# A gated DeltaNet layer: the low products of a weight tile last, and no products with the zero state of a head's first chunk

## The chip, the cores and the metric

The kernel runs on one core of a Trainium2 chip. The metric is the device time of one execution in microseconds (us). Engines: TensorE (PE) multiplies, VectorE (DVE), ScalarE (ACT) and GpSimd (POOL) work elementwise, SyncE (SP) issues the DMAs.

## The reference

DEPTH is 1, so the one layer is the gated DeltaNet: 1024 tokens, width 1024, 8 heads with keys of 128 and values of 256, all in float32.

```python
h = rms_norm(x, norm_w) * (1 + scale) + shift          # shift, scale, gate from c
qkv, z, b, a = split(h @ w_in)
q, k, v = split(silu(causal_short_conv(qkv, conv_w)))   # q, k l2-normed per head
def step(S, inp):                                       # per head, chunk by chunk
    v_new = u_c - w_c @ S
    o_c = q_c @ S + attn_c @ v_new
    S = S * gl_c + k_c.T @ v_new
    return S, o_c
S0 = zeros                                              # the state of a head's first chunk
y = (rms_norm(o, norm_w) * silu(z)) @ w_out
out = rms_norm(x + gate * y, final_norm_w)
```

u and w come from a triangular solve within each chunk: (I + A)^-1 with A from k k^T, the decay and beta.

## The kernel before

Work is cut into 16 units: unit u = 2 hd + par is one half (512 tokens, four chunks of 128) of head hd. The even unit (par 0) is the first half, so its chunk 0 starts with the zero state; the odd unit goes on with the state of the even one. A unit has six tiles of the input projection (k, z0, z1, q, v0, v1; some for the next unit): `project` (L396) computes tile m as h (1024 x 512) by 128 weight columns in bank m % 2, as 24 products of 128x128 by 128x512. Full precision comes from splits into a high and a low part: for each of the eight k, w_hi h_hi, w_hi h_lo and w_lo h_hi. The weight tile lands in w_raw, two slots, loaded by SP. ACT makes w_hi by a rounding copy (L685, `split_hi`), POOL makes w_lo as the difference, in four operations (L1344, `split_lo`), and frees the slot. On even units POOL also scales and splits the two halves of the head's output weights (L1358, L1351), and SP loads these in between.

The order of every engine is written out by hand. On PE (`body`, L511), `fill(n)` puts the next n products of the projection between the dependent steps. Per unit: the merges of the block inverses (`merge_p`, `merge_d`), k and v of the next and this unit turned, then per chunk c:

- ks (L538) = k_c state and qs (L542) = q_c state, each in two passes in the profile;
- fill, x (L550) = u_fin r, where r = v - e ks is DVE's L1107;
- fill, kv (L560) and av (L563), from xs (ACT's scaled x, L756);
- fill. In chunk 0 the fills have 8, 8 and 6 products (`FILLS`, L257), and tile 3 (n = 72) begins with the first of them.

DVE in an even unit (`body`, L1071), behind make_n (L992) for the next unit: memset of the state (L1100), r (L1107), a silu (L947), and the inversion of the next unit's 16x16 blocks, cut into `BASE_STEPS` (L262). Three of its steps, two small operations each (L1007, L1011), come in chunk 0 before the state's update (L1124) and o (L1130), then a silu and three more steps, then r of chunk 1. The inversion's input goes through DRAM: SP, in `body` (L348), waits for wo_lo of the second output half, loads tile 4, then in `invert_out` (L287) stores nmat to n_dram (L289), waits until that has landed and reads it back as blocks (L291). ACT (`body`, L776) in chunk 0: scaled q state (L750), z evacuated (L703, L706), scaled x (L756), then w_hi of tile 4.

Semaphores count per unit: `passed(engine, name, u, n)` waits for the n-th event of that name in unit u. `UNIT` (L155) has the counts: state_done 5 per unit, the first by the memset, or in the odd unit by an increment alone.

Of the kernel before, what the change touches and what calls it, by code (L numbers as in the profile page):

```python
# [7 lines left out]
ALU = mybir.AluOpType  # L8
ACT = mybir.ActivationFunctionType

P = 128
# [4 lines left out]
DV = 256  # L16
# [3 lines left out]
KT = D_MODEL // P  # L20
# [19 lines left out]
def build(nc, x, c, ada_w, ada_b, norm_w, w_in, conv_w, a_log, dt_bias, gdn_norm_w, w_out,  # L40
          final_norm_w, out):
    ctx = ExitStack()
    with ctx:
# [32 lines left out]
        neg_egc = sb("neg_egc", [P, UNITS, NCH])  # L76
        e_kd = sb("e_kd", [P, UNITS, NCH])
        e_gl = sb("e_gl", [P, UNITS, NCH])
# [13 lines left out]
        state = sb("state", [P, DV])  # L92

        def part(at, n, **dims):
# [3 lines left out]
        cvk = part(0, 1024, to="p (s t) -> p s t", s=2)  # L98
# [20 lines left out]
        r_rhs = part(10752, DV)  # L119
# [39 lines left out]
            base_step=32, base_done=1, t_done=1,  # L159
            merge_p=3, merge_p_out=3, merge_d=3, merge_d_out=3,  # L160
            ks_done=4, qs_done=4, r_done=4, qs_scaled=4, x_done=4, x_out=4,
            kv_done=4, av_done=4, state_done=5, o_done=4, o_squared=4, o_step=4, o_pow=4,
            o_turned=4, og_done=4, og_hi_done=4, og_lo_done=4, out_done=4, y_added=4,
        )
        HEAD = ("wo_gated", "wo_hi_done", "wo_lo_done")
# [45 lines left out]
        def passed(eng, name, u, n):  # L211
            value = at(name, u, n)
            if not isinstance(value, int) or value > 0:
                eng.wait_ge(S[name], value)
# [178 lines left out]
        def _(pe):  # L393
            prime(pe, "tensor")

            def project(u, par, first, last, final=False):  # L396
                first_unit = isinstance(u, int) and u == -1
                for n in range(first, last):
                    m, r = divmod(n, MM)
                    k, part_no = divmod(r, 3)  # L400
                    if r == 0:
                        passed(pe, "w_lo_done", u, m + 1)
                        passed(pe, "evacuated", u, m - 1)
                    half = par if final or (m in (1, 2) and not first_unit) else 1 - par
                    w, h = ((w_hi, h_hi_v), (w_hi, h_lo_v), (w_lo, h_hi_v))[part_no]
                    mm = nc.tensor.matmul(bank[m % 2][:, :], w[:, m % 2, k, :], h[:, k, half, :],  # L406
                                          start=(r == 0), stop=(r == MM - 1))
                    if r == MM - 1:
                        mm.then_inc(S["projected"], 1)
# [101 lines left out]
            def body(hd, par, last=False, begun=0, fills=FILLS):  # L511
# [20 lines left out]
                fill(in_v)  # L532

                for c in range(NCH):
                    passed(pe, "state_done", u, c + 1)
                    if c == 0:
                        passed(pe, "v_scaled", u, 4)
                    nc.tensor.matmul(bank[2][:, 0:DV], cvk[:, par, c * P:(c + 1) * P], state[:, :],  # L538
                                     start=True, stop=True).then_inc(S["ks_done"], 1)
                    passed(pe, "og_done", u, max(c - 1, 0))  # L540
                    passed(pe, "qs_scaled", u, c)
                    nc.tensor.matmul(bank[3][:, 0:DV], cvq[:, par, c * P:(c + 1) * P], state[:, :],  # L542
                                     start=True, stop=True).then_inc(S["qs_done"], 1)
                    if c >= 2:
                        out_project(u, c - 2, 0, hd, par, not last)
                    fill(in_chunk[c][0])
                    if c == 0:
                        passed(pe, "merge_d_out", u, 3)
                    passed(pe, "r_done", u, c + 1)
                    nc.tensor.matmul(bank[4][:, 0:DV], u_fin[:, c, :], r_rhs, start=True, stop=True  # L550
                                     ).then_inc(S["x_done"], 1)
                    if c >= 2:
                        out_project(u, c - 2, 1, hd, par, not last)
                    fill(in_chunk[c][1])
# [123 lines left out]
        def _(act):  # L678
# [97 lines left out]
            def body(hd, par, last=False, first=False):  # L776
# [22 lines left out]
                    split_hi(u, hd, par, 3)  # L799
                scale_v(u, par)  # L800
                for c in range(NCH):
                    scale_q(u, c)
                    if not last:
                        if c == 0:
                            evacuate_z(u, 2, 1)
# [102 lines left out]
        def _(dve):  # L908
# [162 lines left out]
            def body(hd, par, last=False, first=False):  # L1071
# [23 lines left out]
                    k_scalars(u + 1, other)  # L1095
                    make_n(u + 1, other)

                if par == 0:
                    passed(dve, "qs_done", u, 0)
                    nc.vector.memset(state[:, :], 0.0).then_inc(S["state_done"], 1)  # L1100
                else:
                    dve.sem_inc(S["state_done"], 1)
                for c in range(NCH):
                    passed(dve, "ks_done", u, c + 1)
                    passed(dve, "v_scaled", u, c + 1)
                    passed(dve, "x_done", u, c)
                    stt(out=r_rhs, in0=bank[2][:, 0:DV], scalar=neg_egc[:, u, c:c + 1], in1=vt[:, c, :],  # L1107
                        op0=ALU.mult, op1=ALU.add).then_inc(S["r_done"], 1)
                    if c == 0:
                        if last:  # L1110
                            silu(u, 1, zt[:, 1, :], gate=True)
# [8 lines left out]
                    if c > 0:  # L1120
                        gate_o(u, c - 1)
                    passed(dve, "kv_done", u, c + 1)
                    passed(dve, "qs_done", u, c + 1)
                    stt(out=state[:, :], in0=state[:, :], scalar=e_gl[:, u, c:c + 1], in1=bank[4][:, DV:2 * DV],  # L1124
                        op0=ALU.mult, op1=ALU.add).then_inc(S["state_done"], 1)
                    passed(dve, "av_done", u, c + 1)
                    passed(dve, "qs_scaled", u, c + 1)
                    passed(dve, "o_turned", u, c - 1)
                    passed(dve, "o_squared", u, c - 1)
                    nc.vector.tensor_tensor(o_raw[:, c % 2, :], bank[5][:, 0:DV], qss, ALU.add  # L1130
                                            ).then_inc(S["o_done"], 1)
                    if c >= 2:
                        add_y(u, par, c - 2)
                    if not last:
# [346 lines left out]
```

## Time and profile before

| | |
|---|---|
| Median of 3 runs | 1201.96 us (1201.87 to 1202.51) |
| The profiled execution | 1203.63 us, its span 1201.8 us |
| PE busy | 1114.4 us, 93% of the span |
| DVE, ACT, POOL busy | 836.7, 448.1, 599.9 us (70, 37, 50%) |
| Mean granted TensorE clock | 0.972 |
| Longest chain | PE 64%, POOL 12%, DVE 11%, issue 7% |
| DMA | 87.73 MB on the one queue, 26.6% of its engines' time |

Busy time is the sum over an engine's instructions in the profile. The chain is followed back from the last instruction to what released each step. Idle time is put down to the instruction whose semaphore came last; idle of an engine that is not the bound costs nothing by itself.

### The profile page before, as it was taken

The page shows a single profiled execution, that of the slowest core. Times are in us where ns is not written, and L with a number is a line of the kernel's source. Part 1 is how long each engine was busy: PE and PEld are TensorE (multiplying, and loading weights), DVE is VectorE, ACT ScalarE, POOL GpSimd, SP SyncE. Part 2 cuts the span into 40 slices and gives each one's busy share as a digit, 9 for nine tenths or more (in the row PEclk, how much of TensorE's full clock was granted, in tenths as well). Part 3 has the DMA queues.
Part 4 walks back from the last instruction along what each step waited for, and adds up shares of the span by engine and source line. Part 5 has one row for each costly group of instructions (what it writes and reads, how often), then busy time and mean ns, then how long its engine had stood idle before and what let it go on. Part 6 is the DMA issues. An engine that isn't in the chain of part 4 may idle for free.

```text
span 1201.8 us, 19507 instructions
## 1 busy us (share of the span) xinstructions
PE 1114.4 (93%) x5628; PEld 920.6 (77%) x5628; DVE 836.7 (70%) x1888; ACT 448.1 (37%) x1038; POOL 599.9 (50%) x819
## 2 busy tenths in 40 slices
PE   3896899999999999999999999999999999999984
PEld 2665688887888788887888788887888788887863
DVE  4776586776858586775858586685868677685835
ACT  4642333333242433433333333334243333334333
POOL 2353544565444744466345754456444853456413
PEclk9897899999999999999999999999999999999988
DMA  9922222213122321223221221223221222213103
GB/s 311 326 58 60 63 58 62 55 57 81 40 62 57 80 57 44 56 60 76 55 62 40 81 65 43 62 55 81 57 59 43 79 56 55 62 40 97 33 25 123
DMA packets 150754, 88.31 MB, mean 73 GB/s; under 512 B 29446, under 2 KB 145320, under 8 KB 150696
## 3 DMA queue, kind: packets, MB, share of 16 engines
q1 hardware_dynamic: 150696, 87.73, 26.6%
q14 instruction: 45, 0.37, 0.1%
q8 instruction: 13, 0.21, 0.1%
HBM read 78.28 MB, written 9.44 MB: 73 GB/s over the span
## 4 chain that ended last, share of the span: by engine, by line
PE 64%; POOL 12%; DVE 11%; issue 7%; ACT 2%; DMA 1%; SPq 0%; DVEq 0%; POOLq 0%; ACTq 0%
PE bank L406 31%; PE bank L506 11%; POOL w_lo L1344 5%; POOL wo_lo L1351 4%; DVE y L963 3%; DVE work L930 3%; PE bank L550 2%; PE bank L466 2%; PE bank L560 2%; PE bank L538 2%; PE bank L542 2%; PE bank L482 2%; PE bank L475 2%; PE bank L563 2%; PE bank L588 1%
## 5 line engine op out<-in xcount | busy, mean ns | idle before, releaser
L1344 POOL TENSOR_TENSOR w_lo<-w_raw,w_hi 128x256 fp32r<-128x256 f32 x384 | 333.5, 898 | 254.9 <-ACT w_hi L685 254.8
L406 PE MATMUL bank<-h_hi,w_hi 128*128 128x512 f32 x760 | 320.2, 421 | 20.8 <-POOL w_lo L1344 20.8
L406 PE MATMUL bank<-h_lo,w_hi 128*128 128x512 f32 x760 | 313.4, 412 | 0.0
L406 PE MATMUL bank<-h_hi,w_lo 128*128 128x512 f32 x760 | 310.6, 409 | 0.0
L406 PEld LDWEIGHTS bank<-h_hi,w_hi 128*128 128x128 f32 x760 | 146.5, 193 | 53.7 <-POOL w_lo L1344 24.8
L930 DVE SCALAR_TENSOR_TENSOR work<-pre,cw,work 128x512 f32<-128x512 f32 x192 | 168.5, 878 | 14.1 <-DVE work L927 5.4
L406 PEld LDWEIGHTS bank<-h_hi,w_lo 128*128 128x128 f32 x760 | 145.6, 192 | 30.8 <-issue 0.2
L406 PEld LDWEIGHTS bank<-h_lo,w_hi 128*128 128x128 f32 x760 | 146.9, 193 | 27.8 <-issue 0.2
L1394 POOL TENSOR_TENSOR og_lo<-work,og_hi 128x256 fp32r<-128x256 f32 x64 | 47.1, 737 | 217.4 <-ACT og_hi L745 217.4
L711 ACT ACTIVATE work<-work 128x512 f32<-128x512 f32 x64 | 40.2, 628 | 271.8 <-DVE pre L940 131.0
L506 PE MATMUL bank<-wo_hi,og_hi 128*128 128x512 f32 x256 | 113.7, 444 | 10.1 <-DVE y L963 10.1
L963 DVE SCALAR_TENSOR_TENSOR y<-bank,o_rs,y 128x512 f32<-128x512 f32 x128 | 89.5, 739 | 23.4 <-PE bank L506 23.4
L1007 DVE TENSOR_TENSOR work<-work 32x15 f32<-32x15 f32 (+7 forms) x240 | 70.1, 292 | 47.0 <-DMA work<-n_dram 39.2
L685 ACT ACTIVATE w_hi<-w_raw 128x1024 fp32r<-128x1024 f32 x96 | 101.2, 1054 | 1.6 <-DMA w_raw<-in_gdn_w_in 1.6
L506 PE MATMUL bank<-wo_hi,og_lo 128*128 128x512 f32 x256 | 100.7, 393 | 0.0
L506 PE MATMUL bank<-wo_lo,og_hi 128*128 128x512 f32 x256 | 100.3, 392 | 0.0
L947 DVE SCALAR_TENSOR_TENSOR work<-work 128x512 f32<-128x512 f32 x96 | 76.7, 799 | 3.2 <-ACT work L711 1.4
L756 ACT ACTIVATE work<-bank,k_tab 128x256 f32<-128x256 f32 x64 | 30.4, 475 | 116.4 <-PE bank L550 116.4
L954 DVE SCALAR_TENSOR_TENSOR work<-bank,small,work 128x128 f32<-128x128 f32 x128 | 38.7, 342 | 50.1 <-PE bank L491 50.1
L745 ACT ACTIVATE og_hi<-work 128x256 fp32r<-128x256 f32 x64 | 26.7, 417 | 115.6 <-DVE work L954 112.6
L506 PEld LDWEIGHTS bank<-wo_hi,og_hi 128*128 128x128 f32 x256 | 48.0, 188 | 24.1 <-POOL og_lo L1394 14.2
L1011 DVE TENSOR_TENSOR work<-work 32x15 f32<-32x15 f32 (+7 forms) x240 | 60.1, 250 | 8.3
(176 smaller groups left out, 1870.0 us busy)
## 6 DMA issues: line engine op xcount, KB each, us to landing
w_raw<-in_gdn_w_in SPq DMA_DIRECT2D x96, 512.0 KB, 4.0
work<-in_ada_w SPq DMA_DIRECT2D x8, 1024.0 KB, 9.7
w_raw<-in_gdn_w_out SPq DMA_DIRECT2D x16, 512.0 KB, 3.3
y<-in_x SPq DMA_DIRECT2D x8, 512.0 KB, 9.1
work<-in_ada_w SPq DMA_DIRECT2D x8, 512.0 KB, 6.1
n_dram<-work SPq DMA_DIRECT2D x16, 256.0 KB, 3.4
out<-y SPq DMA_DIRECT2D x8, 512.0 KB, 2.7
t_dram<-work SPq DMA_DIRECT2D x16, 64.0 KB, 1.6
```

The source lines that it names most:

```text
L406: mm = nc.tensor.matmul(bank[m % 2][:, :], w[:, m % 2, k, :], h[:, k, half, :], start=(r == 0), stop=(r == MM - 1))
L506: mm = nc.tensor.matmul(bank[6 + n][:, :], a[:, m, :], w[:, m, n * 512:(n + 1) * 512], start=(m == 0 and q == 0), stop=(m == 1 and q == 2))
L685: nc.scalar.activation(w_hi[:, k % 2, :, :], w_raw_k[:, k % 2, :, :], ACT.Copy).then_inc(S["w_hi_done"], 1)
L711: nc.scalar.activation(th[:, m % 2, :], cv, ACT.Tanh, scale=0.5).then_inc(S["tanh_done"], 1)
L930: o = stt(out=cv, in0=pre[:, r, j:j + HALF], scalar=tap, in1=cv, op0=ALU.mult, op1=ALU.add)
L947: stt(out=t, in0=th[:, m % 2, :], scalar=1.0, in1=t, op0=ALU.add, op1=ALU.mult).then_inc(S["silu_done"], 1)
L963: i = stt(out=yt, in0=bank[6 + n][:, :], scalar=o_rs[:, c:c + 1], in1=yt, op0=ALU.mult, op1=ALU.add)
L1007: nc.vector.tensor_tensor(tmp, blk_n[:, j:j + 1, j + 1:].rearrange("p o n -> p n o").to_broadcast(shape), blk_y[:, j:j + 1, 0:j + 1].to_br ...
L1011: nc.vector.tensor_tensor(below, below, tmp, ALU.subtract).then_inc(S["base_step"], 1)
L1344: i = nc.gpsimd.tensor_tensor(w_lo[:, k % 2, j:j + 2, :], w_raw_k[:, k % 2, j:j + 2, :], w_hi[:, k % 2, j:j + 2, :].bitcast(F32), ALU.subt ...
L1351: o = nc.gpsimd.tensor_tensor(wo_lo[:, i, j:j + 256], w_raw[:, 1 - i, j:j + 256], wo_hi[:, i, j:j + 256].bitcast(F32), ALU.subtract)
L1394: nc.gpsimd.tensor_tensor(og_lo[:, :, :], og, og_hi[:, :, :].bitcast(F32), ALU.subtract).then_inc(S["og_lo_done"], 1)
```

## The change

In `project` the 24 products of a tile come in another order: first, for each k, w_hi h_hi and w_hi h_lo (r = 0 to 15), then for each k w_lo h_hi (r = 16 to 23). At r = 0 PE waits for w_hi and the bank, and only at r = 16 for w_lo. In the first chunk of an even unit ("fresh") ks and qs are left out, x takes the scaled v in place of r, DVE makes no r and no memset, and copies kv to the state and av to o; ACT leaves out the scaled q state. Semaphores are incremented instead where something counts them. state_done has 4 events a unit.

```diff
--- before.py
+++ after.py
@@ -159,7 +159,7 @@
             base_step=32, base_done=1, t_done=1,
             merge_p=3, merge_p_out=3, merge_d=3, merge_d_out=3,
             ks_done=4, qs_done=4, r_done=4, qs_scaled=4, x_done=4, x_out=4,
-            kv_done=4, av_done=4, state_done=5, o_done=4, o_squared=4, o_step=4, o_pow=4,
+            kv_done=4, av_done=4, state_done=4, o_done=4, o_squared=4, o_step=4, o_pow=4,
             o_turned=4, og_done=4, og_hi_done=4, og_lo_done=4, out_done=4, y_added=4,
         )
         HEAD = ("wo_gated", "wo_hi_done", "wo_lo_done")
@@ -397,10 +397,13 @@
                 first_unit = isinstance(u, int) and u == -1
                 for n in range(first, last):
                     m, r = divmod(n, MM)
-                    k, part_no = divmod(r, 3)
+
+                    k, part_no = divmod(r, 2) if r < 2 * KT else (r - 2 * KT, 2)
                     if r == 0:
+                        passed(pe, "w_hi_done", u, m + 1)
+                        passed(pe, "evacuated", u, m - 1)
+                    elif r == 2 * KT:
                         passed(pe, "w_lo_done", u, m + 1)
-                        passed(pe, "evacuated", u, m - 1)
                     half = par if final or (m in (1, 2) and not first_unit) else 1 - par
                     w, h = ((w_hi, h_hi_v), (w_hi, h_lo_v), (w_lo, h_hi_v))[part_no]
                     mm = nc.tensor.matmul(bank[m % 2][:, :], w[:, m % 2, k, :], h[:, k, half, :],
@@ -532,23 +535,29 @@
                 fill(in_v)
 
                 for c in range(NCH):
-                    passed(pe, "state_done", u, c + 1)
+                    fresh = par == 0 and c == 0
                     if c == 0:
                         passed(pe, "v_scaled", u, 4)
-                    nc.tensor.matmul(bank[2][:, 0:DV], cvk[:, par, c * P:(c + 1) * P], state[:, :],
-                                     start=True, stop=True).then_inc(S["ks_done"], 1)
-                    passed(pe, "og_done", u, max(c - 1, 0))
-                    passed(pe, "qs_scaled", u, c)
-                    nc.tensor.matmul(bank[3][:, 0:DV], cvq[:, par, c * P:(c + 1) * P], state[:, :],
-                                     start=True, stop=True).then_inc(S["qs_done"], 1)
+                    if fresh:
+                        pe.sem_inc(S["ks_done"], 1)
+                        pe.sem_inc(S["qs_done"], 1)
+                    else:
+                        passed(pe, "state_done", u, c)
+                        nc.tensor.matmul(bank[2][:, 0:DV], cvk[:, par, c * P:(c + 1) * P], state[:, :],
+                                         start=True, stop=True).then_inc(S["ks_done"], 1)
+                        passed(pe, "og_done", u, max(c - 1, 0))
+                        passed(pe, "qs_scaled", u, c)
+                        nc.tensor.matmul(bank[3][:, 0:DV], cvq[:, par, c * P:(c + 1) * P], state[:, :],
+                                         start=True, stop=True).then_inc(S["qs_done"], 1)
                     if c >= 2:
                         out_project(u, c - 2, 0, hd, par, not last)
                     fill(in_chunk[c][0])
                     if c == 0:
                         passed(pe, "merge_d_out", u, 3)
-                    passed(pe, "r_done", u, c + 1)
-                    nc.tensor.matmul(bank[4][:, 0:DV], u_fin[:, c, :], r_rhs, start=True, stop=True
-                                     ).then_inc(S["x_done"], 1)
+                    if not fresh:
+                        passed(pe, "r_done", u, c + 1)
+                    nc.tensor.matmul(bank[4][:, 0:DV], u_fin[:, c, :], vt[:, 0, :] if fresh else r_rhs,
+                                     start=True, stop=True).then_inc(S["x_done"], 1)
                     if c >= 2:
                         out_project(u, c - 2, 1, hd, par, not last)
                     fill(in_chunk[c][1])
@@ -799,7 +808,10 @@
                     split_hi(u, hd, par, 3)
                 scale_v(u, par)
                 for c in range(NCH):
-                    scale_q(u, c)
+                    if par == 0 and c == 0:
+                        act.sem_inc(S["qs_scaled"], 1)
+                    else:
+                        scale_q(u, c)
                     if not last:
                         if c == 0:
                             evacuate_z(u, 2, 1)
@@ -1095,17 +1107,17 @@
                     k_scalars(u + 1, other)
                     make_n(u + 1, other)
 
-                if par == 0:
-                    passed(dve, "qs_done", u, 0)
-                    nc.vector.memset(state[:, :], 0.0).then_inc(S["state_done"], 1)
-                else:
-                    dve.sem_inc(S["state_done"], 1)
                 for c in range(NCH):
-                    passed(dve, "ks_done", u, c + 1)
-                    passed(dve, "v_scaled", u, c + 1)
-                    passed(dve, "x_done", u, c)
-                    stt(out=r_rhs, in0=bank[2][:, 0:DV], scalar=neg_egc[:, u, c:c + 1], in1=vt[:, c, :],
-                        op0=ALU.mult, op1=ALU.add).then_inc(S["r_done"], 1)
+
+                    fresh = par == 0 and c == 0
+                    if fresh:
+                        dve.sem_inc(S["r_done"], 1)
+                    else:
+                        passed(dve, "ks_done", u, c + 1)
+                        passed(dve, "v_scaled", u, c + 1)
+                        passed(dve, "x_done", u, c)
+                        stt(out=r_rhs, in0=bank[2][:, 0:DV], scalar=neg_egc[:, u, c:c + 1], in1=vt[:, c, :],
+                            op0=ALU.mult, op1=ALU.add).then_inc(S["r_done"], 1)
                     if c == 0:
                         if last:
                             silu(u, 1, zt[:, 1, :], gate=True)
@@ -1120,15 +1132,22 @@
                     if c > 0:
                         gate_o(u, c - 1)
                     passed(dve, "kv_done", u, c + 1)
-                    passed(dve, "qs_done", u, c + 1)
-                    stt(out=state[:, :], in0=state[:, :], scalar=e_gl[:, u, c:c + 1], in1=bank[4][:, DV:2 * DV],
-                        op0=ALU.mult, op1=ALU.add).then_inc(S["state_done"], 1)
+                    if fresh:
+                        passed(dve, "qs_done", u, 0)
+                        nc.vector.tensor_copy(state[:, :], bank[4][:, DV:2 * DV]).then_inc(S["state_done"], 1)
+                    else:
+                        passed(dve, "qs_done", u, c + 1)
+                        stt(out=state[:, :], in0=state[:, :], scalar=e_gl[:, u, c:c + 1], in1=bank[4][:, DV:2 * DV],
+                            op0=ALU.mult, op1=ALU.add).then_inc(S["state_done"], 1)
                     passed(dve, "av_done", u, c + 1)
-                    passed(dve, "qs_scaled", u, c + 1)
                     passed(dve, "o_turned", u, c - 1)
                     passed(dve, "o_squared", u, c - 1)
-                    nc.vector.tensor_tensor(o_raw[:, c % 2, :], bank[5][:, 0:DV], qss, ALU.add
-                                            ).then_inc(S["o_done"], 1)
+                    if fresh:
+                        nc.vector.tensor_copy(o_raw[:, 0, :], bank[5][:, 0:DV]).then_inc(S["o_done"], 1)
+                    else:
+                        passed(dve, "qs_scaled", u, c + 1)
+                        nc.vector.tensor_tensor(o_raw[:, c % 2, :], bank[5][:, 0:DV], qss, ALU.add
+                                                ).then_inc(S["o_done"], 1)
                     if c >= 2:
                         add_y(u, par, c - 2)
                     if not last:
```

PE, chunk 0 of an even unit in the loop, before: from ks to x ("..." stands for six more products of the tile).

```order
L538 MATMUL bank<-state,work 128x256 [waits v_scaled,state_done]
L542 MATMUL bank<-state,work 128x256 [waits qs_scaled,og_done]
L214 REGISTER_ALU
L406 MATMUL bank<-h_hi,w_hi 128x512 [waits evacuated,w_lo_done]
L406 MATMUL bank<-h_lo,w_hi 128x512
L406 MATMUL bank<-h_hi,w_lo 128x512
...
L214 REGISTER_ALU [waits merge_d_out]
L550 MATMUL bank<-work 128x256 [waits r_done]
```

And with the change, from the wait for the scaled v to ks of chunk 1:

```order
L214 REGISTER_ALU [waits v_scaled]
L409 MATMUL bank<-h_hi,w_hi 128x512 [waits evacuated,w_hi_done]
L409 MATMUL bank<-h_lo,w_hi 128x512
...
L559 MATMUL bank<-work 128x256 [waits merge_d_out]
...
L569 MATMUL bank<-work 128x256 [waits kdec_done,x_out]
L572 MATMUL bank<-work 128x256 [waits o_done]
L409 MATMUL bank<-h_hi,w_lo 128x512 [waits w_lo_done]
L409 MATMUL bank<-h_hi,w_lo 128x512 x5
L546 MATMUL bank<-state,work 128x256 [waits state_done]
```

L538 and L542 are gone from this place; the wait for w_lo_done stands behind L569 and L572 (L560 and L563 of before), on the first of the six products of the third fill, and the next wait is L546's for state_done.

DVE, the same chunk, before: from make_n to the first inversion step.

```order
L992 SCALAR_TENSOR_TENSOR work<-bank,k_tab,work 128x128 x3
L1100 MEMSET state 128x256 [waits qs_done]
L1107 ISA [waits x_done,v_scaled,ks_done]
L1107 SCALAR_TENSOR_TENSOR work<-bank,neg_egc,work 128x256
...
L947 SCALAR_TENSOR_TENSOR work<-work 128x512 [waits evacuated,tanh_done]
...
L214 REGISTER_ALU [waits blk_in]
L1007 TENSOR_TENSOR work<-work 32x15 [waits base_step]
```

And with the change, from make_n to o:

```order
L1004 SCALAR_TENSOR_TENSOR work<-bank,k_tab,work 128x128 x3
...
L959 SCALAR_TENSOR_TENSOR work<-work 128x512 [waits evacuated,tanh_done]
...
L214 REGISTER_ALU [waits blk_in]
L1019 TENSOR_TENSOR work<-work 32x15 [waits base_step]
...
L1023 TENSOR_TENSOR work<-work 32x13x3 [waits base_step]
L1137 COPY state<-bank 128x256 [waits qs_done,kv_done]
L214 REGISTER_ALU [waits av_done]
L1146 COPY work<-bank 128x256 [waits o_squared,o_turned]
```

The memset and r, and their waits, are gone; the wait for blk_in (the reload of n_dram) and the inversion's six operations stand ahead of the state's copy as they stood ahead of its update.

## Rows read from the trace of the kernel before

**Rows 1.** Who waited for whom: us in total, times, longest (us).
```profile
DVE work L1007 <- DMA work<-n_dram: 39.2, 8, 5.2
...
PE bank L406 <- POOL w_lo L1344: 20.8, 10, 2.3
```

**Rows 2.** Timeline of PE, u = 8 (start us, us, engine line op, idle before).
```profile
547.15 0.60 PE L538 MATMUL bank<-state,work 128*128 128x256 f32 x2
...
550.46 0.80 PE L406 MATMUL bank<-h_hi,w_hi 128*128 128x512 f32 x1 [2.29 <-POOL w_lo L1344]
...
558.44 0.60 PE L538 MATMUL bank<-state,work 128*128 128x256 f32 x2
...
561.16 0.65 PE L550 MATMUL bank<-work 128*128 128x256 f32 x2
```

**Rows 3.** Windows, two even units (length, engines' busy, PEclk, DMA, GB/s).
```profile
550.30:553.60 3.30, 3.14 (x7) 2.51 (x8) 0.00 (x0) 0.00 (x0) 0.11 (x1) 0.50 0.52 145
1096.30:1099.60 3.30, 3.23 (x8) 2.55 (x9) 0.00 (x0) 0.00 (x0) 0.02 (x1) 0.52 0.46 130
```

**Rows 4.** Timeline of PE in an odd unit, u = 7.
```profile
480.55 0.60 PE L538 MATMUL bank<-state,work 128*128 128x256 f32 x2
...
481.64 0.40 PE L406 MATMUL bank<-h_lo,w_hi 128*128 128x512 f32 x1
481.88 0.40 PE L406 MATMUL bank<-h_hi,w_lo 128*128 128x512 f32 x1
...
487.79 0.59 PE L538 MATMUL bank<-state,work 128*128 128x256 f32 x2
```

**Rows 5.** Timeline of DVE in u = 8.
```profile
554.38 0.17 DVE L1007 TENSOR_TENSOR work<-work 32x15 f32<-32x15 f32 x1 [4.82 <-DMA work<-n_dram]
...
555.44 0.19 DVE L1011 TENSOR_TENSOR work<-work 32x39 f32<-32x39 f32 x1
556.91 0.48 DVE L1124 SCALAR_TENSOR_TENSOR state<-state,e_gl,bank 128x256 f32<-128x256 f32 x1 [1.29 <-PE bank L560]
...
558.63 0.72 DVE L1007 TENSOR_TENSOR work<-work 32x48 f32<-32x48 f32 x1
...
560.57 0.48 DVE L1107 SCALAR_TENSOR_TENSOR work<-bank,neg_egc,work 128x256 f32<-128x256 f32 x1
```

**Rows 6.** Timeline of POOL in u = 8.
```profile
544.40 2.84 POOL L1351 TENSOR_TENSOR wo_lo<-w_raw,wo_hi 128x256 fp32r<-128x256 f32 x4
...
556.04 3.26 POOL L1344 TENSOR_TENSOR w_lo<-w_raw,w_hi 128x256 fp32r<-128x256 f32 x4 [5.63 <-ACT w_hi L685]
```

**Rows 7.** SP's issues in u = 8; the first's time to landing (last row, us).
```profile
547.26 0.38 SPq L269 DMA_DIRECT2D w_raw<-in_gdn_w_in  x1
547.75 0.52 SPq L289 DMA_DIRECT2D n_dram<-work  x1
552.36 0.34 SPq L291 DMA_DIRECT2D work<-n_dram  x1
...
w_raw<-in_gdn_w_in SPq DMA_DIRECT2D x1, 512.0 KB, 4.4
```

**Rows 8.** Timeline of ACT in u = 8.
```profile
554.91 1.05 ACT L685 ACTIVATE w_hi<-w_raw 128x1024 fp32r<-128x1024 f32 x1
```

**Rows 9.** Timeline of DVE in an odd unit, u = 7; POOL's L1344 ends at 498.62.
```profile
497.35 0.67 DVE L1011 TENSOR_TENSOR work<-work 32x60 f32<-32x60 f32 x1
...
498.73 0.20 DVE L1011 TENSOR_TENSOR work<-work 32x55 f32<-32x55 f32 x1
```

**Rows 10.** Timeline of PE in the start, and the window 122 to 123 us.
```profile
83.20 0.51 PE L406 MATMUL bank<-h_hi,w_hi 128*128 128x512 f32 x1 [1.68 <-POOL w_lo L1344]
...
110.43 1.97 PE L466 MATMUL bank<-work 128*128 128x64 f32 x8 [7.49 <-DVE work L1028]
114.16 0.79 PE L406 MATMUL bank<-h_hi,w_hi 128*128 128x512 f32 x1 [1.76 <-POOL w_lo L1344]
...
122.00:123.00 1.00, 1.00 (x7) 0.99 (x5) 0.00 (x0) 0.00 (x0) 1.00 (x2) 0.50 0.07 12
```

## The prediction

> **What bounds the kernel now.** I began with the page: TensorE (PE) is busy nearly all of the span, so the time is what PE's stream costs plus its waits. Next came the list of who waited for whom [rows 1]. PE waited 20.8 us in 10 waits for GpSimd's low half of a weight tile (L1344), and VectorE (DVE) 39.2 us in 8 waits for the reload of n_dram.
>
> The timeline of PE in the even unit of one head, u = 8 [rows 2], shows the stall: behind the two products with the state (the first at 547.15), 2.29 us pass until tile 3's first product. The same stands in all eight even units; two of the ten waits lie in the start (1.68 and 1.76 us [rows 10]), so the eight have (20.8 - 3.44) / 8 = 2.17 us on the mean. The windows [rows 3] add what idle time hides: behind the stall the granted clock is 0.50 (1.2 of 2.4 GHz) for 3.3 us, in the last such unit as in this one. At half clock 1.65 us of work are lost. A stall costs 2.17 + 1.65.
>
> **The change, part by part.** In PE's order the low products of a tile, and their wait, come behind the sixteen high ones. Tile 3's then stand behind L560 and L563 of chunk 0.
> - Stall. PE reaches them at about 552.1 (547.15 and the odd unit's spacing, less the state products). w_lo(3) is there by 550.46 [rows 2], so this stall goes, with 1.6 us to spare. w_hi(3) is no new wait: ScalarE makes it ahead of the scaled v that PE waits for at this place already.
> - State products. They cost 1.09 us from 480.55 to 481.64, less one normal product (0.24, 481.64 to 481.88): 0.86 us [rows 4].
> - With no other wait, ks of chunk 1 would come 7.24 us (480.55 to 487.79 in the odd unit, which has no stall) less 0.86 behind 547.15: at 553.53, against 558.44 now. That is 4.91 us earlier per head, if nothing else is late.
>
> **What is late next.** ks of chunk 1 reads the state, and DVE writes the state behind the first three inversion steps of the next unit, which wait for n_dram [rows 5]. They start at 554.38 and end at 555.63; the state follows at 556.91, since it waits 1.29 us for L560. The slack is that 1.3 us, not 4.9. And 554.38 doesn't move. SP issues tile 4's load at 547.26, when POOL's wo_lo (L1351) ends at 547.24 [rows 6], then n_dram's store at 547.75, and the reload when that has landed, at 552.36 [rows 7]. All of this starts ahead of the part of PE's stream that gets shorter. So the stall moves to L546 (L538 of before).
>
> **A collision.** Now w_hi(4) starts at 554.91, behind L550's result [rows 8], and POOL's w_lo(4) at 556.04, when the three steps are done [rows 6]. With L550 at about 549, ScalarE waits only for the tile, landed 4.4 us behind its issue [rows 7]: w_hi(4) 551.7 to 552.8, w_lo(4) 552.9 to 555.7. The three steps then run beside POOL. In the odd unit such an operation beside L1344 takes 0.67 us, and 0.20 when POOL is done [rows 9]. The Trainium skill ("GPSIMD Engine Reference", Specifications) says that GpSimd shares its SBUF interfaces with VectorE and contends with instructions that have two SBUF inputs. By that rule the steps are held and the state's, from PSUM, is not; the trace agrees (0.72 against 0.48 for L1124, both beside L1344) [rows 5].
> Bounds of the delay: 0 (POOL done first), and all six operations at 0.68 instead of 0.21, 2.8 us. I take two held turns, 1.2 us, since POOL would be in the last two of its four operations.
>
> **The sum for a head.** Steps end at 556.85, the state takes 0.48 (at most, L1124's), 0.1 to start: ks at 557.4, 1.04 us earlier than now. PE has stood since 553.7: 3.7 us. The eight stalls of about 2.2 us halved the clock, so this one does: 1.65 us lost. From ks to L550 are 2.72 us (558.44 to 561.16), so L550 of chunk 1 is at 561.8, not 561.16: **+0.6 us**. DVE's r (560.57 now, 3.66 behind the state's start, of which 0.8 was spent beside POOL) is there at 560.3 and doesn't bind. Two additions. DVE no longer waits for ks and runs its silu beside POOL's last wo_lo operation, on which the DMA chain hangs: bounds 0 and 0.3, I take 0.1. And the clock can stay low longer: in the start it still stood at 0.50 at 122 us though PE worked from 114.16 on [rows 10]; here a longer gap can reach into the slow stretch in the same way. Bounds 0 and 1.65; one head in five, 0.3 on the mean. Together +1.0 us, for 7 heads **+7.0**.
>
> **The start and the rest.** The wait at 83.20 is worth nothing, since PE then waits 7.49 us for DVE at 110.43. The 1.76 us at 114.16 go, and the merge products behind them start what DVE does next: -1.8, to -3 if the clock comes back sooner [rows 10]. In the first even unit I take 0. The reordered products are the same in number and kind. The removed memset, scale and r of the first chunk lie in the shadow of the DMA; the added semaphore increments on PE, ACT and DVE lie ahead of the new gap, so at up to a few tenths each they cost nothing.
> Sum: 7.0 - 1.8 = +5.2 us. The profiled execution took 1203.63 (span 1201.8); the median of the runs, 1201.96, lies 1.7 lower, and the sum is added to it: **1207.0 us** (A).
>
> **Rivals.**
> - **B, gain.** POOL's w_lo(4) doesn't hold the steps: ks at 556.2, gap 2.5, clock halved, L550 at 560.57. That is -0.6 for 8 heads, start -2.4: 1194.8. For it: 1.2 us is my choice between 0 and 2.8. Against: the tile lands 0.7 us ahead of n_dram, and the reload takes 2 us more. It decides below some 0.6 us of delay.
> - **B2, as B with the clock kept.** r at 559.9 then holds L550: -1.3 for 8 heads, start -2.4: 1189.2. At 83.20 a gap of 1.68 us was followed by a product of 0.51 us, at 550.46 one of 2.29 by 0.80 [rows 2, 10], and this gap would be the longer. The Trainium skill ("TensorE: Matmul & The Clock Gate", Why this matters for your kernels) warns only of gaps longer than all eight stalls. By that rule B2 would stand in B's place; the clock of all eight speaks against it.
> - **D, a second slow stretch in every head.** +0.6 + 0.1 + 1.5 for 7 heads, less 1.8: 1215.6.
> - **N, they cancel.** Delay 0.7: ks at 556.9, with the additions +0.2 for 8 heads, start -1.8: 1201.8.
> - **F, nothing is late next.** 8 (2.17 + 1.65 + 0.86) = 37.4, start 2.4: 1162.2. That the change doesn't move the wait is excluded by the order; for its whole gain the reload would have to land 3 us sooner.
>
> **How the numbers follow.** Chances: A 0.48 (its own range 1203 to 1211), B 0.17, B2 0.08, D 0.12, N 0.12, F 0.03. "Same" is within 0.2%, 2.4 us, about what a measurement of this kernel can tell. Slower: 0.44 of A and D, 0.56. Same: 0.04 of A and 0.11 of N. Faster: B, B2, F and 0.01 of N, 0.29. The range leaves out B2, F and the upper half of D: 1194 to 1215. Both signs hold weight, since 0.6 us per head changes them.
>
> **What would show it.** The waits of PE's projection for L1344 fall from 10 to 1 or 0. In their place stand 8 waits of the state product for DVE's state copy, 3.3 to 4 us each, and a DVE idle of 6 to 7 us ahead of the inversion's first step, still ended by n_dram. L1344 for tile 4 starts some 1.5 us ahead of that step, and the first two operations take 0.5 to 0.7 us. The clock is 0.50 behind each gap. It is wrong if the gap is under 2.7 us (B), if the clock stays at 1.00 (B2), if operations beside POOL take 0.2 us, or if PE waits at L550's successor in chunk 1 for r instead.

## The result and the profile after

| | before | after |
|---|---|---|
| Median of the runs taken together | 1201.87 us (5 runs, 1200.05 to 1202.51) | 1207.0 us (5 runs, 1206.86 to 1207.17) |
| Profiled execution, its span | 1203.63, 1201.8 us | 1206.86, 1204.4 us |
| PE busy | 1114.4 us | 1108.6 us |
| POOL, DVE busy | 599.9, 836.7 us | 600.9, 833.0 us |
| Mean granted clock | 0.972 | 0.971 |

The ratio is 1.0046 (95% interval 1.0036 to 1.0057): slower by 5 us, though PE's busy time fell by 5.8 us.

Who waited for whom, after (us in total, times, longest), against [rows 1]:

```profile
PE bank L546 <- DVE state L1137: 25.1, 8, 3.8
...
PE bank L469 <- DVE work L1040: 9.2, 1, 9.2
...
DVE work L1019 <- DMA work<-n_dram: 56.6, 8, 7.5
```

No product of the projection waits for w_lo any more. Its 20.8 us in 10 waits are replaced by 25.1 us in 8, of the second chunk's ks (L546) for the state that DVE copies (L1137). DVE's idle ahead of the reload has grown from 39.2 to 56.6 us.

PE after, single products left out, against [rows 2]. It is the same even unit, the fourth, at about 550 us; by the kernel's own count from 0 that is u = 6, not 8 as the rows ahead call it (and their odd unit is u = 5), and it is called u = 6 from here on:

```profile
547.73 0.60 PE L559 MATMUL bank<-work 128*128 128x256 f32 x2
...
550.68 1.74 PE L409 MATMUL bank<-h_hi,w_lo 128*128 128x512 f32 x6
555.91 1.22 PE L546 MATMUL bank<-state,work 128*128 128x256 f32 x2 [3.50 <-DVE state L1137]
...
561.20 0.92 PE L559 MATMUL bank<-work 128*128 128x256 f32 x2
```

The low products run at 550.68 without a wait, and PE then stands 3.50 us. In the seven heads from u = 2 to u = 14 the gap is 3.39 to 3.79 us, in the first even unit (145.67) 0.34.

DVE, POOL, ACT and SP in the same unit, against [rows 5 to 8]:

```profile
544.92 0.85 DVE L959 SCALAR_TENSOR_TENSOR work<-work 128x512 f32<-128x512 f32 x1
...
553.53 0.45 DVE L1019 TENSOR_TENSOR work<-work 32x15 f32<-32x15 f32 x1 [7.36 <-DMA work<-n_dram]
554.01 0.65 DVE L1023 TENSOR_TENSOR work<-work 32x15 f32<-32x15 f32 x1
554.70 0.18 DVE L1019 TENSOR_TENSOR work<-work 32x28 f32<-32x28 f32 x1
...
555.34 0.19 DVE L1023 TENSOR_TENSOR work<-work 32x39 f32<-32x39 f32 x1
555.45 0.41 DVE L1137 COPY state<-bank 128x256 f32<-128x256 f32 x1
```

```profile
543.07 3.29 POOL L1370 TENSOR_TENSOR wo_lo<-w_raw,wo_hi 128x256 fp32r<-128x256 f32 x4
546.32 2.81 POOL L1363 TENSOR_TENSOR w_lo<-w_raw,w_hi 128x256 fp32r<-128x256 f32 x4
551.86 2.77 POOL L1363 TENSOR_TENSOR w_lo<-w_raw,w_hi 128x256 fp32r<-128x256 f32 x4 [2.72 <-ACT w_hi L694]
```

```profile
550.72 1.06 ACT L694 ACTIVATE w_hi<-w_raw 128x1024 fp32r<-128x1024 f32 x1 [1.88 <-DMA w_raw<-in_gdn_w_in]
```

```profile
546.38 0.38 SPq L269 DMA_DIRECT2D w_raw<-in_gdn_w_in  x1
546.87 0.52 SPq L289 DMA_DIRECT2D n_dram<-work  x1
551.45 0.34 SPq L291 DMA_DIRECT2D work<-n_dram  x1
```

The first two inversion operations lie in w_lo(4)'s last 1.1 us and take 0.45 and 0.65 us; from 554.70 on, with POOL idle, they take 0.18. The silu (L959), with two small memsets behind it, lies beside wo_lo, which now takes 3.29 us where it took 2.84 [rows 6], and SP's load, store and reload hang on its end.

Windows after, behind the stall of u = 6 and of u = 10, against [rows 3] (length, busy of PE, PEld, DVE, ACT, POOL, then clock, DMA, GB/s):

```profile
555.90:559.30 3.40, 3.38 (x8) 2.72 (x9) 3.09 (x13) 1.41 (x4) 0.73 (x2) 0.50 0.60 152
...
831.60:835.00 3.40, 3.36 (x8) 2.72 (x9) 3.10 (x13) 1.38 (x4) 0.73 (x2) 0.51 0.60 154
```

**One zero of time for all kernels.** ks(c) is the first product with the state in chunk c (L538 before, L546 after). In an even unit DVE's first operation of the k_tab (L978 before, L990 after) lies ahead of all that changed there but the order of the products, so times from its start, E, can be compared: 543.23 before and 541.90 after in u = 6. Means over the seven heads from u = 2 to u = 14:

| us | E to ks(1) | ks(1) to ks(2) | E to the next head's E |
|---|---|---|---|
| before | 15.28 | 7.52 | 136.57 |
| after | 14.10 | 9.49 | 137.63 |

So ks of chunk 1 comes 1.18 us sooner, but at half clock: what follows takes 1.97 us more, for a slow stretch (a time at a granted clock of 0.50) begins around it. In five heads it takes 9.05 to 9.17 us, in u = 6 and u = 12, where the clock stays at 0.50 for 6.8 us instead of 3.4, 10.36 and 10.49. The other 0.3 us lies in the rest of the head. A head costs 1.06 us more.

### The profile page after: what moved, and what is told of

The parts are those of the page before. It is cut to its first block, busy times and chain, and to the rows that moved or that the text cites. A ratio compares the mean times of both kernels' runs of the same rounds, so it can differ in the third digit from the quotient of the medians.

```text
span 1204.4 us, 19318 instructions
## 1 busy us (share of the span) xinstructions
PE 1108.6 (92%) x5596; PEld 914.4 (76%) x5596; DVE 833.0 (69%) x1872; ACT 446.6 (37%) x1030; POOL 600.9 (50%) x819
## 4 chain that ended last, share of the span: by engine, by line
PE 60%; DVE 15%; POOL 10%; issue 6%; DMA 5%; ACT 2%; SPq 1%; DVEq 1%; POOLq 0%; ACTq 0%
PE bank L409 26%; PE bank L509 11%; POOL wo_lo L1370 4%; DVE work L942 3%; DVE y L975 3%; DMA n_dram<-work 3%; PE bank L469 2%; PE bank L546 2%; POOL w_lo L1363 2%; PE bank L559 2%; PE bank L550 2%; PE bank L569 2%; PE bank L485 2%; PE bank L478 2%; POOL w_raw L1377 1%
## 5 line engine op out<-in xcount | busy, mean ns | idle before, releaser
L1363 POOL TENSOR_TENSOR w_lo<-w_raw,w_hi 128x256 fp32r<-128x256 f32 x384 | 326.5, 881 | 232.5 <-ACT w_hi L694 232.5
L409 PE MATMUL bank<-h_hi,w_hi 128*128 128x512 f32 x760 | 329.3, 433 | 2.0 <-ACT work L748 2.0
L409 PE MATMUL bank<-h_lo,w_hi 128*128 128x512 f32 x760 | 302.9, 399 | 0.0
L409 PE MATMUL bank<-h_hi,w_lo 128*128 128x512 f32 x760 | 207.6, 405 | 0.0
L942 DVE SCALAR_TENSOR_TENSOR work<-pre,cw,work 128x512 f32<-128x512 f32 x192 | 168.3, 877 | 14.1 <-DVE work L939 5.4
L1019 DVE TENSOR_TENSOR work<-work 32x15 f32<-32x15 f32 (+7 forms) x240 | 69.1, 288 | 64.6 <-DMA work<-n_dram 56.6
L959 DVE SCALAR_TENSOR_TENSOR work<-work 128x512 f32<-128x512 f32 x96 | 76.2, 794 | 2.9 <-ACT work L720 1.0
L1023 DVE TENSOR_TENSOR work<-work 32x15 f32<-32x15 f32 (+7 forms) x240 | 64.4, 268 | 8.3
L469 PEld LDWEIGHTS bank<-work 128*128 128x128 f32 x384 | 52.0, 197 | 20.2 <-DVE work L1040 9.6
```

The source lines that it names most:

```text
L469: mm = nc.tensor.matmul(p_bank[:, c, :, :], nmat[:, c, :], pairs(tm, lv)[:, c, :, 0, :], start=True, stop=True)
L942: o = stt(out=cv, in0=pre[:, r, j:j + HALF], scalar=tap, in1=cv, op0=ALU.mult, op1=ALU.add)
L959: stt(out=t, in0=th[:, m % 2, :], scalar=1.0, in1=t, op0=ALU.add, op1=ALU.mult).then_inc(S["silu_done"], 1)
L1019: nc.vector.tensor_tensor(tmp, blk_n[:, j:j + 1, j + 1:].rearrange("p o n -> p n o").to_broadcast(shape), blk_y[:, j:j + 1, 0:j + 1].to_br ...
L1023: nc.vector.tensor_tensor(below, below, tmp, ALU.subtract).then_inc(S["base_step"], 1)
L1363: i = nc.gpsimd.tensor_tensor(w_lo[:, k % 2, j:j + 2, :], w_raw_k[:, k % 2, j:j + 2, :], w_hi[:, k % 2, j:j + 2, :].bitcast(F32), ALU.subt ...
```

## The experiments

Each ratio is to the kernel before on the same chip, with its 95% interval. An edit is to the changed kernel where nothing else is said.

**1. low_last**: the kernel before with only the order of the products and their waits changed; the state products stay.

```diff
-                    k, part_no = divmod(r, 3)
+                    k, part_no = divmod(r, 2) if r < 2 * KT else (r - 2 * KT, 2)
```

The waits go with it as in the change, and in the next edit back.

> Only the low products last, with their wait; the products with the zero state stay. Theory A (the state of chunk 0 waits for three inversion steps, these for the reload of n_dram, and the gap before ks of chunk 1 halves the clock): ks and qs are back, so PE comes 0.86 us later to the same gap, 2.3 to 2.8 us instead of 3.5; wo_lo isn't held by the silu, which again waits for ks; POOL's w_lo(4) still runs beside the first steps (+0.75). ks of chunk 1 some 1.5 us earlier than before, 1.65 lost in slow clock: +0.1 to +0.2 us per head, the start -3: 1198 to 1202 us. Rival 1 (the new order of the products costs time by itself): 1207 or more, and mean product times above before's. Rival 2 (a removed stall is simply saved, 2.17 + 1.65 for 8 heads): 1171.

**2. no_zero_state**: only the fresh chunk; the old product order.

```diff
-                    k, part_no = divmod(r, 2) if r < 2 * KT else (r - 2 * KT, 2)
+                    k, part_no = divmod(r, 3)
```

> Only the products with the zero state (and their r, scale and memset) left out, the old order of the products. Theory A: the wait for w_lo(3) takes the 0.86 us back: 8 waits of about 3.0 instead of 2.2 us, clock halved behind them as before, the state behind L560 as before: 1200 to 1204 us. Rival 1: 1202 as well, or less by 7 (0.86 for 8 heads) if those products were on the path: 1195. Rival 2: 1195.

Measured: low_last 1198.4 us, 0.9973 (0.9963 to 0.9983); no_zero_state 1205.54 us, 1.0035 (1.0026 to 1.0045). PE's waits of the one, and of the other:

```profile
PE bank L540 <- DVE state L1126: 18.6, 10, 2.5
```

```profile
PE bank L407 <- POOL w_lo L1361: 25.0, 9, 3.2
```

The order alone replaces the wait for w_lo by one for the state of 2.0 to 2.6 us, with the same 3.4 us at half clock behind it: the loop gains nothing (136.8 us a head against 136.57). What is won lies ahead of it (E of u = 2 at 266.07 us, before at 269.69) and behind it (from E of u = 14 to the end 1.6 us less), where a slow stretch of before is missing in the last unit. The rival that the order itself costs time falls. The fresh chunk alone brings PE 0.9 us sooner to a wait whose end doesn't move: 2.9 to 3.2 us instead of 2.17. What it saves on PE is idle time later. Its result is 1.5 us above its range. In the profiled execution (1206.71 us) one of the seven heads has a slow stretch of 6.8 us, worth 1.4 us; another 1.0 us is lost ahead of u = 2 and 1.0 in the rest of the loop, and for these no cause is shown.

**3. n_first**: in the even units SP stores and reloads n_dram ahead of its wait for wo_lo and of tile 4's load.

```diff
+                    invert_out(u + 1)
                     wo_passed(sp, "wo_lo_done", hd, 2)
                     load_tile(0, v_cols(nxt, 0))
...
-                invert_out(u + 1)
+                    invert_out(u + 1)
```

The last line keeps it in the odd units where it was.

> The changed kernel, and in even units SP stores n_dram and reads it back before it waits for wo_lo and loads tile 4. Theory A: the reload lands at about 549 instead of 553.5, ahead of the kv product, so the gap before ks of chunk 1 goes and with it the slow clock: 4.5 to 6 us per head against the changed kernel, 1160 to 1172 us; mean granted clock 0.99. Rival 1 and any cause in PE's own order or in the added increments: 1205 to 1207. If only the collision with w_lo(4) made the gap: about 1202.

**4. steps_late**: SP as it was; in the even units DVE's first six inversion steps stand behind r of chunk 1.

```diff
+                        if par == 0 and c == 1:
+                            invert_blocks(u + 1, 0, 9)
+                        elif not fresh:
+                            invert_blocks(u + 1, *BASE_STEPS[c])
```

The call for steps 3 to 5, behind chunk 0's second silu, is left to the odd units in the same way.

> The changed kernel, and in even units DVE does the first six inversion steps behind r of chunk 1 instead of in chunk 0; SP's order stays. Theory A: the state is written right behind the kv product, no gap before ks of chunk 1, clock kept; nine steps then stand between r and the state of chunk 1, 4 to 5 us, which may give a wait of up to 1 us before ks of chunk 2: 1160 to 1178 us. Rival 1: 1205 to 1207. If the reload itself were waited for elsewhere on PE: above 1195.

Measured: 1169.76 us, 0.9738 (0.9722 to 0.9754), and 1170.55 us, 0.9746 (0.973 to 0.9763). SP, then PE and DVE of n_first in u = 6:

```profile
537.64 0.38 SPq L289 DMA_DIRECT2D n_dram<-work  x1
539.96 0.34 SPq L291 DMA_DIRECT2D work<-n_dram  x1
```

```profile
543.36 1.73 PE L410 MATMUL bank<-h_hi,w_lo 128*128 128x512 f32 x6
544.93 0.59 PE L547 MATMUL bank<-state,work 128*128 128x256 f32 x2
```

```profile
541.98 0.17 DVE L1020 TENSOR_TENSOR work<-work 32x15 f32<-32x15 f32 x1 [3.20 <-DMA work<-n_dram]
```

One edit brings the reload sooner, the other takes the state out from behind it, and both take away the same stall: ks(1) comes 10.4 us behind E instead of 14.1, with no gap, and the clock stays at 1.00 through the loop. A head takes 132.0 and 132.2 us, and both times lie in their ranges. That the state's place behind the reload makes the stall is shown. Without tile 4's load ahead of it the store is done 2.32 us behind its issue, instead of 4.58 (546.87 to 551.45 above).

**5. n_first_before**: SP's new order in the kernel before.

> The kernel before, with only SP's order changed: in the even units it stores and reloads n_dram ahead of its wait for wo_lo and of tile 4's load. Theory A (in the kernel before the reload hides behind the wait for w_lo(3); it is the change that brings it onto the path): VectorE's idle ahead of the steps falls by about 3 us per head, PE's eight waits for w_lo(3) stay at 2.0-2.3 us, and the time is 1199-1203 us. Rival (the reload bound the kernel before as well): 1185-1195 us.

Measured: 1199.3 us, 0.9984 (0.9972 to 0.9997).

```profile
PE bank L407 <- POOL w_lo L1345: 19.5, 10, 2.6
```

```profile
DVE work L1008 <- DMA work<-n_dram: 7.4, 8, 1.2
```

DVE's idle for the reload falls from 39.2 to 7.4 us, and the time hardly moves: PE waits for w_lo as before. The same edit is worth 2 us here and 37 us in the changed kernel.

**6. lo4_after_state**: POOL makes w_lo(4) of an even unit only when the state is there.

```diff
+                        if par == 0:
+                            passed(pool, "state_done", u, 1)
                         split_lo(u, 4)
```

> The change, and GpSimd waits in the even units for the first chunk's state before it makes w_lo(4), so that no operation of GpSimd lies beside the first six inversion steps. Theory A (the steps are held by w_lo(4), 2.0 us instead of 1.25): the steps take 1.25 us, the stall at ks of chunk 1 falls from 3.4-3.8 to 2.6-3.0 us, and 7 heads save about 0.75 us each: 1200-1204 us, ratio to before 0.998 to 1.002. Rival (the steps are slow for another reason, or ks is bound by something else): unchanged, 1206-1208 us. A gap of 2.7 us should still be followed by a stretch at granted clock 0.50; if it is not, 1190-1194 us.

**7. silu_after_wo**: DVE waits in the fresh chunk for the second wo_lo ahead of its silu.

```diff
+                        if fresh:
+                            wo_passed(dve, "wo_lo_done", hd, 2)
```

> The change, and VectorE waits in the first chunk of the even units for GpSimd's second wo_lo before its silu, so that wo_lo is made alone. Theory A (the silu beside it holds wo_lo, 3.29 us instead of 2.84, and the loads behind it): wo_lo takes 2.84 us, SP's load, n_dram's store and the reload come 0.4 us sooner, and 7 heads save about 0.4 us each: 1202-1206 us. Rival (the chain store-reload is set by the DMA queue, not by wo_lo's end): unchanged, 1206-1208 us.

**8. both_apart**: both waits.

> Both waits: no operation of GpSimd beside the silu or beside the steps. Theory A: the gains add, 1.1 to 1.2 us per head, about 8 us: 1198-1202 us; the stall at ks of chunk 1 is 2.2-2.6 us and the clock behind it is still 0.50. If the clock keeps at 1.00 behind it: 1187-1191 us. Rival (only one of the two matters): 1202-1206 us.

Measured, and from the traces the means over the seven heads:

| | us | ratio | E to ks(1) | a head |
|---|---|---|---|---|
| the change | 1207.0 | 1.0046 (1.0036 to 1.0057) | 14.10 | 137.63 |
| lo4_after_state | 1204.26 | 1.0021 (1.0009 to 1.0033) | 13.31 | 136.81 |
| silu_after_wo | 1205.46 | 1.0027 (1.0012 to 1.0042) | 13.87 | 137.22 |
| both_apart | 1201.16 | 0.9996 (0.9985 to 1.0007) | 13.06 | 136.70 |

Taking the two collisions away gives back 0.8 and 0.2 to 0.4 us a head, and both together 0.93 of the 1.06 us that a head had lost. lo4_after_state ended 0.3 us above its range. But w_lo(4) pushed back falls on DVE's next operations, in both_apart as well: in all seven heads of these two runs r of chunk 1 begins 4.1 us behind ks(1), and 2.2 in the changed kernel. So a collision is moved and not removed, and what the change is worth without any wasn't measured. PE, DVE and the window behind the stall of lo4_after_state in u = 6:

```profile
559.31 0.70 PE L546 MATMUL bank<-state,work 128*128 128x256 f32 x2 [2.89 <-DVE state L1137]
...
563.98 0.70 PE L559 MATMUL bank<-work 128*128 128x256 f32 x2 [1.69 <-DVE work L1119]
```

```profile
560.12 0.73 DVE L1019 TENSOR_TENSOR work<-work 32x48 f32<-32x48 f32 x1
560.88 0.66 DVE L1023 TENSOR_TENSOR work<-work 32x48 f32<-32x48 f32 x1
...
563.44 0.49 DVE L1119 SCALAR_TENSOR_TENSOR work<-bank,neg_egc,work 128x256 f32<-128x256 f32 x1
```

```profile
559.30:563.90 4.60, 2.98 (x12) 2.18 (x12) 4.40 (x10) 1.47 (x4) 4.07 (x6) 1.00 0.03 9
```

Here the clock stays at 1.00, and still nothing is won beyond the collision: r (L1119), held behind four operations of 0.65 to 0.73 us, makes PE wait 1.69 us more. From ks(1) to ks(2) are 9.5 us in the two heads at half clock and in the five at full clock alike. I had expected 0.50 behind these gaps, or 1190 to 1194 us for a clock that is kept. Both were wrong: PE, at full clock, has to wait for r.

**9. n_first_low_last**: the kernel before with n_first's order of SP and low_last's order of the products; the products with the zero state stay, in DVE's and ACT's code too.

> The reordered low products with the zero-state products kept, and SP stores and reloads n_dram ahead of the wait for wo_lo and of tile 4's load. Theory: with the reload sooner the state never binds, so this differs from the full change with the same SP order (1169.8 us) by the state products alone: 8 x 0.86 = 6.9 us, 1175-1178 us, no stall in the loop. Rival (the state products lay in a shadow there, worth nothing): 1169-1171 us. If the later memset and state of this version bind, 1180-1195 us.

Measured: 1182.77 us (1177.85 to 1183.69), 0.9839 (0.9821 to 0.9857).

```profile
PE bank L553 <- DVE work L1110: 6.6, 9, 0.9
```

```profile
545.70 2.82 POOL L1347 TENSOR_TENSOR w_lo<-w_raw,w_hi 128x256 fp32r<-128x256 f32 x4 [4.15 <-ACT w_hi L688]
```

```profile
545.74 0.74 DVE L1014 TENSOR_TENSOR work<-work 32x48 f32<-32x48 f32 x1
546.52 0.67 DVE L1010 TENSOR_TENSOR work<-work 32x55 f32<-32x55 f32 x1
547.22 0.66 DVE L1014 TENSOR_TENSOR work<-work 32x55 f32<-32x55 f32 x1
547.91 0.67 DVE L1010 TENSOR_TENSOR work<-work 32x60 f32<-32x60 f32 x1
548.62 0.21 DVE L1014 TENSOR_TENSOR work<-work 32x60 f32<-32x60 f32 x1
548.85 0.48 DVE L1110 SCALAR_TENSOR_TENSOR work<-bank,neg_egc,work 128x256 f32<-128x256 f32 x1
```

Against n_first the fresh chunk is worth 13 us, not 7: a head takes 133.75 us instead of 131.98. 0.96 us of the difference lie ahead of ks(1), about the two products. Another 1.0 us lies between ks(1) and ks(2), and it is this wait of x(1) for r. The rows of u = 6 show why: w_lo(4) begins 0.1 us behind ks(1) (545.60) and holds four of DVE's operations ahead of r. In n_first PE reaches ks(1) sooner (544.93), w_lo(4) begins 0.8 us behind it, and two are held; over the seven heads it is four each time here and none to two there. The start gives 4 us back (ks(1) of u = 0 at 144.27, in n_first at 148.03). The profiled execution took 1178.84 us, so the traces explain 9 us; what the 4 us more of three of the five runs are stays open.

## Why the prediction was right

The forecast was A, 1207.0 us, and the runs gave 1207.0. That they agree to the tenth is luck: the mechanism in the loop held, but its terms were off by more, in both directions, and the account of the start was wrong.

- **The stall goes.** Right: no wait for w_lo. With w_hi(3) there was no new wait either.
- **It comes back at ks(1), for the state behind the steps.** Right, and shown by n_first and steps_late. Expected were eight gaps of 3.3 to 4 us and a DVE idle of 6 to 7; there are seven of 3.4 to 3.8 and one of 0.34, and the idle is 7.36 in u = 6.
- **554.38 doesn't move.** Off by 0.5 us: in time from E the steps began at 11.15 us and begin at 11.63 (553.53 - 541.90); the means of the seven heads are 11.29 and 11.65. The term that failed is the silu beside wo_lo: I took 0.1, with a bound of 0.3, and it was 0.45 (3.29 against 2.84). In silu_after_wo wo_lo takes 2.84 again and SP's load comes the whole 0.45 us sooner. Only 0.2 us of it arrive at ks(1), since n_dram's store then took 4.84 us on the mean instead of 4.64 until the reload's issue; why is open.
- **The collision of w_lo(4) with the steps.** The mechanism was right, to the operations: POOL began w_lo(4) 1.67 us ahead of the first step (expected: 1.5), and the first two operations were held. The size wasn't: I took 1.2 us for two held turns. The six operations with their gaps took 2.00 us (553.53 to 555.53) instead of 1.25: 0.75 us, and 0.8 on the mean.
- **ks(1) 1.04 us sooner.** It was 1.18, since the two errors above nearly cancel (on the mean the steps began 0.3 us later than I took, and were held 0.4 less).
- **Half clock behind each gap, 1.65 us.** Right: the clock falls to 0.50 in all seven heads of the loop, and costs 1.6 us in five.
- **A second slow stretch in one head of five.** Two of seven, 1.3 us each: 0.4 a head where I took 0.3. D (every head) fell.
- **+1.0 us a head.** +1.06, of which 0.3 lies in the rest of the head, which I had no term for.
- **The start, -1.8, and the first even unit, 0.** Together they are -2.5 (E of u = 2 at 267.16 against 269.69), but it lies the other way round. The wait of 1.76 us for w_lo goes, but PE then stands 4.22 us instead of 1.60 for DVE's silu, and works at half clock again from 125.0 to 131.7 us. So E of u = 0 comes only 0.6 us sooner (133.04 against 133.62), and PE begins chunk 0 there at 137.13 instead of 137.25. The clock doesn't come back sooner in sum either: between 104 and 133 us the mean granted clock is 0.71 both times. The gain is made in the first even unit itself, whose wait of 2.03 us for w_lo and state products are gone while ks(1) waits 0.34 us only, with the clock at 1.00 behind it; part of its chunk 0 ran at half clock ahead of that, which brought PE there later. Before, then after:

```profile
129.53 0.66 PE L415 MATMUL bank<-ident,work 128*128 128x128 f32 x4 [1.60 <-DVE work L947]
137.25 0.67 PE L538 MATMUL bank<-state,work 128*128 128x256 f32 x2 [1.75 <-ACT work L739]
140.38 0.53 PE L406 MATMUL bank<-h_hi,w_hi 128*128 128x512 f32 x1 [2.03 <-POOL w_lo L1344]
```

```profile
126.81 1.11 PE L418 MATMUL bank<-ident,work 128*128 128x128 f32 x4 [4.22 <-DVE work L959]
137.13 0.47 PE L409 MATMUL bank<-h_hi,w_hi 128*128 128x512 f32 x1 [2.05 <-ACT work L748]
145.67 0.70 PE L546 MATMUL bank<-state,work 128*128 128x256 f32 x2 [0.34 <-DVE state L1137]
```

- **The end.** I had no term. In the last unit PE waits 1.75 us for ACT's scaled v before and 1.66 after. Before, the clock is at 0.50 behind it for 6.8 us; after, not. Whether that is the change's doing isn't shown: in no_zero_state the clock fell for 6.8 us behind the same wait of 1.66.

```profile
1157.69 1.01 PE L538 MATMUL bank<-state,work 128*128 128x256 f32 x2 [1.75 <-ACT work L739]
```

```profile
1158.00:1164.00 6.00, 5.43 (x13) 3.25 (x12) 1.98 (x4) 1.26 (x3) 0.00 (x0) 0.50 0.00 0
```

```profile
1161.90 0.70 PE L546 MATMUL bank<-state,work 128*128 128x256 f32 x2 [1.66 <-ACT work L748]
```

```profile
1162.00:1168.00 6.00, 4.66 (x16) 2.52 (x16) 2.47 (x5) 2.70 (x7) 0.84 (x3) 1.00 0.01 1
```

So the spans differ by -2.5 + 6 x 1.06 - 1.3 = +2.6 us, where I had +5.2: six periods lie between the seven heads' E, and the last head with the end gives 1.3 back. The medians differ by 5.1, since the profiled execution of before lay 1.8 us above its median, that of after at its own. One longer slow stretch is worth 1.3 us, half of the difference between the spans, so of the sum only the +1 us a head is shown well, and it has two of them in it.

**The rivals.** B (a gain, w_lo(4) not in the way) decided below 0.6 us of delay; the delay was 0.75. lo4_after_state, with no delay of the steps, gave 1204.26, not 1194.8: ks(1) came 2.0 us sooner than before instead of 2.2, what follows took 2.0 us more instead of 1.65, since r was held, and the rest of the head's 0.3 was missing. B2 (the clock kept) happened in five heads of lo4_after_state and gave nothing there, but with w_lo(4) on r's path, which B2 didn't have; B2 as it was meant stays untested. The Trainium skill ("TensorE: Matmul & The Clock Gate", Why this matters for your kernels) warns only of longer gaps than those of before; all eight of those and low_last's, of 2.0 to 2.6 us, were followed by a clock of 0.50. N's sum is what both_apart measured (1201.16 against 1201.8), though with w_lo(4) moved and not gone. F is n_first: 1169.8, against the 1162.2 worked out for it. In the loop nearly its whole gain was there (4.59 us a head of 4.68), once the reload came sooner, as the prediction said; the first head and what lies ahead of it gave nothing (E of u = 2 at 270.01 us, before at 269.69), where F had some 7.

## What to carry to other kernels

Ahead of taking a wait off the bounding engine, ask of the next operation that it will reach sooner what it needs, and follow that back to what doesn't move: here a DMA that was issued behind an engine's wait, hidden by the stall in question. Try the change together with the edit that moves this cover: alone the two were worth +5 and -2 us, together -31. And where engines are packed against one another, taking out work (the silu's wait for ks) also moves operations onto each other; price each such pair from a pair in the trace, in both directions. Ask also where a group that is pushed away will land: w_lo(4) fell on the first steps in the changed kernel and on those ahead of r in lo4_after_state, both_apart and n_first_low_last.

## What the runs showed of the hardware that was not expected

- The length of a gap doesn't tell whether the clock falls. It fell to 0.50 behind gaps of 2.0 to 2.6 us (low_last, seven of seven) and of 3.4 to 3.8 (after, seven of seven). In lo4_after_state it stayed at 1.00 behind gaps of 2.60 to 2.89 in five of seven heads, and fell behind 2.87 and 2.99; in both_apart it stayed behind gaps of 2.34 and 2.47 and fell behind 2.40 and 2.48; and in the last unit it stayed behind 1.66 us in the changed kernel and fell behind 1.66 in no_zero_state. It doesn't fall at a fixed point of the gap either: in the changed kernel it was 0.50 from 0.8 us ahead of the gap's end on in u = 6 (window 555.10 to 555.90), and still 1.00 for the 0.8 us behind it in u = 14 (1107.13 to 1107.93). A slow stretch in the loop lasted 3.4 or 6.8 us each time. What decides between them is open.
- When VectorE and GpSimd meet, either can be held; what decides isn't shown. A 32x15 operation of DVE took 0.65 us instead of 0.17 and POOL's group 2.77; beside the 128x512 silu DVE's took 0.85 instead of 0.67 and POOL's group 3.29 instead of 2.84. The copy of the state from PSUM took 0.41 us, with GpSimd idle beside it.
- A store of 256 KB to DRAM issued 0.5 us behind a 512 KB load was done after 4.58 us, with nothing ahead of it after 2.32.
